# An MLP whose second product keeps partial sums in PSUM and fills four output blocks directly, and GpSimd without its gate at unit 1

## The reference

```python
def rmsnorm(x, g):
    y = xf * lax.rsqrt(jnp.mean(xf * xf, axis=-1, keepdims=True) + EPS)
    return (y * g.astype(jnp.float32)).astype(x.dtype)

def ffn(h, w1, w2):
    return jnp.square(jax.nn.relu(h @ w1)) @ w2

for layer in range(DEPTH):
    ...                                     # mixer, residual add
    hp = hp + ffn(rmsnorm(hp, norm_ffn[layer]), w_ffn1[layer], w_ffn2[layer])
    hs = hs + ffn(rmsnorm(hs, norm_ffn[layer]), w_ffn1[layer], w_ffn2[layer])
y_prompt = rmsnorm(hp, norm_final)
```

## Time and profile before

| | us |
|---|---|
| median of 3 runs | 2751.97 |
| runs, lowest to highest | 2749.49 to 2754.66 |
| profiled execution | 2746.19 |
| its span, first to last instruction | 2744.5 |
| TensorE busy | 2639.2 (96%) |
| VectorE busy | 1495.5 (54%) |
| GpSimd busy | 1447.0 (53%) |
| ScalarE busy | 946.2 (34%) |
| granted TensorE clock, mean | 0.990 |

### The profile page before, as it was taken

The page is one execution under the profiler, slowest core; times in us unless marked ns, Lnnn a source line. Parts: engine busy times, 40 slices in busy tenths (PEclk is TensorE's granted clock), DMA queues, the critical chain, the costliest instruction groups (busy, mean ns, idle before and its releaser), DMA issues. The chain is left out here.

```text
span 2744.5 us, 54327 instructions
## 1 busy us (share of the span) xinstructions
PE 2639.2 (96%) x22779; PEld 2521.7 (92%) x22779; DVE 1495.5 (54%) x1849; ACT 946.2 (34%) x1644; POOL 1447.0 (53%) x912
## 2 busy tenths in 40 slices
PE   8999989999999999999999998899999999999988
PEld 8999978986777799999999998899998999999988
DVE  5112186775554317455576769327336554676677
ACT  4100044656666324333333332211134333334332
POOL 6332201100001456777688888443548777688884
PEclk9999999999999999999999999999999999999999
DMA  6111243320204623344554431311223435554331
GB/s 194 47 48 63 93 145 109 95 77 2 94 2 140 234 74 139 116 163 153 184 213 146 155 117 31 131 47 47 94 108 108 148 113 166 201 216 152 126 109 63
DMA packets 197276, 319.98 MB, mean 117 GB/s; under 512 B 10813, under 2 KB 125250, under 8 KB 193898
## 3 DMA queue, kind: packets, MB, share of 16 engines
q1 hardware_dynamic: 186586, 293.37, 32.1%
q0 software_dynamic: 4032, 14.68, 1.5%
q10 hardware_dynamic: 6416, 8.45, 0.9%
HBM read 228.99 MB, written 91.67 MB: 117 GB/s over the span
## 5 line engine op out<-in xcount | busy, mean ns | idle before, releaser
L932 PE MATMUL psum<-part_hi,whl 128*128 128x258 f32 x3136 | 515.2, 286 | 23.8 <-DVE xlo_plain L1204 14.7
L932 PEld LDWEIGHTS psum<-part_hi,whl 128*128 128x128 f32 x3136 | 438.5, 191 | 27.5 <-DVE xlo_plain L1204 15.4
L478 PE MATMUL psum<-xhi,whl 128*128 128x344 f32 x1776 | 329.2, 320 | 1.1 <-ACT vCs L1367 0.6
L908 PE MATMUL psum<-shi,whl 128*128 128x258 f32 x1920 | 324.4, 283 | 2.2 <-DVE xlo_plain L1167 2.2
L932 PE MATMUL psum<-part_lo,whl 128*128 128x258 f32 x1568 | 317.0, 284 | 0.0
L449 POOL TENSOR_TENSOR whl<-wraw,zeroc 128x1024 fp32r<-128x1024 f32 x62 | 121.3, 1957 | 354.3 <-PE psum L478 169.0
L478 PEld LDWEIGHTS psum<-xhi,whl 128*128 128x128 f32 x1776 | 288.3, 188 | 1.7 <-issue 1.7
L908 PEld LDWEIGHTS psum<-shi,whl 128*128 128x128 f32 x1920 | 271.6, 190 | 2.6 <-POOL whl L353 2.6
L908 PE MATMUL psum<-xhi,whl 128*128 128x258 f32 x1440 | 250.5, 286 | 10.0 <-ACT xlo_plain L1047 10.0
L932 PEld LDWEIGHTS psum<-part_lo,whl 128*128 128x128 f32 x1568 | 244.8, 191 | 0.0
L353 POOL TENSOR_TENSOR whl<-raw_even,whl 128x512 fp32r<-128x512 f32 x112 | 175.5, 1581 | 86.3 <-ACT whl L974 62.2
(11 more groups left out here) (519 smaller groups left out, 5509.9 us busy)
## 6 DMA issues: line engine op xcount, KB each, us to landing
part_raw<-b_spill SPq DMA_DIRECT2D x98, 516.0 KB
b_spill<-rows_H SPq DMA_DIRECT2D x78, 516.0 KB, 3.9
rows<-in_cache_cmp_kv SPq DMA_DIRECT2D x128, 128.0 KB, 2.6
raw_even<-in_w_ffn SPq DMA_DIRECT2D x16, 1024.0 KB, 6.5
out_even<-in_w_ffn SPq DMA_DIRECT2D x16, 1024.0 KB, 6.2
out_odd<-in_w_ffn SPq DMA_DIRECT2D x16, 1024.0 KB, 7.7
raw_odd<-in_w_ffn SPq DMA_DIRECT2D x14, 1024.0 KB, 7.2
wraw<-in_w_in_ab SPq DMA_DIRECT2D x26, 512.0 KB, 3.6
```

What stands on the lines that cost most here:

```text
L478: last = pe.matmul(psum[:, 3 * bset + c, 0:TC], w, rhs[ah][:, k0 + k, c * TC:(c + 1) * TC], start=(k == 0 and n == 0), stop=(k == kn - 1 a ...
L908: last = pe.matmul(psum[:, 2 * pair + h, 0:QT], fast_weights(first, u, i, wh)[:, k, :], fast_operand(i, ah)[:, k, h * QT:(h + 1) * QT], st ...
L932: last = pe.matmul(psum[:, 2 * p + h, 0:QT], out_weights(first, n, wh)[:, k, p % 2, :], (part_hi, part_lo)[ah][x][:, k, h * QT:(h + 1) * Q ...
```

## The change

- `ORDER` becomes 0, 4, 6, 1, 2, 3, 5 and `PARTS` follows it. Block products 0, 4, 6, 1 are added up in PSUM, and so are 3 and 5: only products at places 0, 4 and 5 of a chunk start a new sum. VectorE writes each state after a product into one of four output blocks (`BLOCK`), as a copy for the first four of chunk 0 and as an addition otherwise.
- The joins on VectorE and GpSimd are gone, also GpSimd's wait for them ahead of the plain weights. Layer 1's last row is scaled from its output block.
- GpSimd's second sum goes to a scratch tile (`second_sum`), free once unit 15's product 0 is done, and the order of its parts is new.
- A plain tile is finished in PSUM: sum, factor and residual, the last into `hT`. `f_res` is gone; TensorE waits for `f_h`.
- In the first product GpSimd's order of a unit is low0, low1, low2, s1, low3, s3, s2, low4, s4, low5, low6, without the gate at unit 1. ScalarE's `high(1, 2)` stands right behind `high(1, 1)`.
- In unit 15 VectorE splits operand part 1 ahead of the last square.

```diff
@@ pool_fast
-                if u == 1:
-                    pool.wait_ge(sD, dve_at(layer, "s4_3"))
                 low(0, a11)
                 low(1, a22)
+                low(2, a12)
                 total("low1", a22, a21, a22, ALU.add)
+                low(3, a22)
                 total("s1", a21, a11, a21, ALU.subtract)
                 total("s3", a11, a22, a11, ALU.subtract)
-                low(2, a12)
-                total("low2", a12, a12, a11, ALU.subtract)
-                pool.wait_ge(v_pool, pool_at(layer, f"{u}.s4"))
-                low(3, a22)
                 low(4, a11)
+                total("s2", a12, a12, a11, ALU.subtract)
                 low(5, a12)
                 low(6, a21)
@@ pool_out
-                low(c, 1, 0)
-                low(c, 1, 1)
                 low(c, 0, 0)
                 low(c, 0, 1)
                 for g in range(2):
                     a11, a12, a21, a22 = blocks_[g]
-                    total(c, g, "low1", a22, a21, a22, ALU.add)
-                    total(c, g, "s1", a21, a11, a21, ALU.subtract)
-                    pool.wait_ge(v_pool, pool_at(layer, f"c{c}.low0_{g}"))
-                    total(c, g, "s3", a11, a22, a11, ALU.subtract)
+                    total(c, g, "low0", a11, a11, a21, ALU.subtract)
+                    if c == 0:
+                        pool.wait_ge(v_done, product_done(layer, 15, 0))
+                    total(c, g, "s3", second_sum(g), a22, a11, ALU.subtract)
                     low(c, 4, g)
...
-            pool.wait_ge(sD, dve_at(layer, "m6_4_3"))
-            pool.tensor_tensor(total_of(4), total_of(4), total_of(0), ALU.add).then_inc(v_pool, 1)
-            plain_low(0)
...
+            for q in range(8):
                 plain_low(q)
@@ orders
-        ORDER = (1, 0, 4, 6, 3, 2, 5)
-        PARTS = ("T4", "B11", "T2", "T3", "T1", "B21", "B22")
+        ORDER = (0, 4, 6, 1, 2, 3, 5)
+        PARTS = ("B11", "T2", "T3", "T4", "B21", "T1", "B22")
@@ places
+        BLOCK = {0: (0, 0), 4: (0, 1), 6: (1, 1), 1: (1, 0), 2: (0, 0), 3: (1, 1), 5: (0, 1)}
+        BEFORE = {2: 0, 5: 4, 3: 6}
+        AFTER = {0: 2, 4: 5, 6: 3, 1: 1}
@@ pe_ffn
-                                                     start=(k == 0 and m == 0), stop=(k == 1 and m == 2))
+                                                     start=(k == 0 and m == 0 and o in (0, 4, 5)),
+                                                     stop=(k == 1 and m == 2), skip_group_check=True)
...
-                    pe.wait_ge(f_res, F0 + 8 * layer + q - 1)
+                    pe.wait_ge(f_h, F0 + 8 * layer + q - 1)
@@ act_ffn
             high(1, 0)
             high(1, 1)
+            high(1, 2)
             sums_high(S_T1, "s1_3")
...
-            high(1, 2)
             first_relu(0)
@@ dve_ffn, the products
-                    if c == 0:
+                    if c == 0 and i not in BEFORE:
                         event(dve.tensor_copy(quarters(out_total(i, p)), two_banks(p)))
                     else:
-                        dve.wait_ge(sD, dve_at(layer, f"m{c - 1}_{i}_{p}"))
...
+                        if i in BEFORE:
+                            dve.wait_ge(sD, dve_at(layer, f"m{c}_{BEFORE[i]}_{p}"))
+                        else:
+                            dve.wait_ge(sD, dve_at(layer, f"m{c - 1}_{AFTER[i]}_{p}"))
...
-                if j == 44:
-                    dve.wait_ge(sD, dve_at(layer, "m6_0_3"))
-                    event(dve.tensor_tensor(total_of(2), total_of(2), total_of(0), ALU.add))
...
@@ dve_ffn, the tiles
-                dve.tensor_tensor(thirds(row), thirds(row), pset(n % 2), ALU.add).then_inc(f_res, 1)
-                dve.wait_ge(f_res, F0 + 8 * layer + n + 1)
-                s, v = link("dve", dve.tensor_tensor(row, row, fwide[:, :], ALU.mult))
+                dve.wait_ge(sD, dve_at(layer, f"m6_{(5, 3)[n % 2]}_{p}"))
+                s, v = link("dve", dve.tensor_tensor(pset(n % 2), pset(n % 2), thirds(out_row(n)), ALU.add))
+                dve.wait_ge(s, v)
+                s, v = link("dve", dve.tensor_tensor(pset(n % 2), pset(n % 2), thirds(fwide[:, :]), ALU.mult))
                 dve.wait_ge(s, v)
                 dve.wait_ge(s_reload[p], 32 if layer == 0 else 64)
-                dve.tensor_tensor(hT[:, n, :], hT[:, n, :], row, ALU.add).then_inc(f_h, 1)
+                dve.tensor_tensor(thirds(hT[:, n, :]), thirds(hT[:, n, :]), pset(n % 2), ALU.add).then_inc(f_h, 1)
@@ n_products_by_k
-                        pe.wait_ge(f_res, 7 + t // 3 + F0)
+                        pe.wait_ge(f_h, 7 + t // 3 + F0)
```

More of the change, by code:

```diff
@@ L391, in pool_out @@
             for c in range(7):
-                blocks_ = [[out_block(first, c, i, g) for i in (0, 2, 6, 1)] for g in range(2)]
-                low(c, 1, 0)
-                low(c, 1, 1)
+                blocks_ = [[out_block(first, c, i, g) for i in (0, 2, 3, 1)] for g in range(2)]
                 low(c, 0, 0)
@@ L729, in dve_mlp @@
                 order += ["g0"] if u == 15 else []
[L730 to L731 removed]
+                order += [f"c12_{u}", f"square0_{u}", f"u3_{u}", f"c21_{u}", f"c22_{u}"]
+                order += ["g1"] if u == 15 else []
+                order += [f"square1_{u}"]
+                order += [f"{x}_{u // 2}" for x in ("T1", "T2", "T4", "T3")] if u % 2 and u < 15 else []
             for j in range(49):
@@ L737, in dve_mlp @@
                 order += {47: ["g49", "g50"], 48: ["g52"]}.get(j, [f"g{j + 2}"])
-                order += {86 // 2 + 1: ["e11"], 86 // 2 + 2: ["e12a"], 86 // 2 + 3: ["e12b"]}.get(j, [])
             return order
-        POOL_UNIT = ("low0", "low1", "s1", "s3", "s2", "low2", "s4", "low3", "low4", "low5", "low6")
-        POOL_OUT = ("low1_0", "low1_1", "low0_0", "low0_1", "s1_0", "s3_0", "s2_0", "low4_0", "s1_1", "s3_1", "s2_1",
-                    "low4_1", "low6_0", "low6_1", "low3_0", "low3_1", "low2_0", "s4_0", "low2_1", "s4_1", "low5_0", "low5_1")
+        POOL_UNIT = ("low0", "low1", "low2", "s1", "low3", "s3", "s2", "low4", "s4", "low5", "low6")
+        POOL_OUT = ("low0_0", "low0_1", "s3_0", "s2_0", "low4_0", "s3_1", "s2_1", "low4_1", "low6_0", "low6_1",
+                    "low1_0", "low1_1", "s1_0", "s1_1", "low2_0", "s4_0", "low2_1", "s4_1", "low3_0", "low3_1", "low5_0", "low5_1")
         def pool_mlp():
@@ L747, in pool_mlp @@
             order += [f"c{c}.{x}" for c in range(7) for x in POOL_OUT]
-            order += ["V", "plain0", "U3", "plain1", "plain2", "plain3", "C21_0", "C22_0", "plain4", "plain5"]
-            order += [f"{x}_{p}" for p in range(1, 4) for x in ("C21", "C22")]
-            return order + ["plain6", "plain7", "scaled", "with_residual"]
+            return order + [f"plain{q}" for q in range(8)] + ["scaled", "with_residual"]
         def act_at(layer, name):
```

97 lines of the change are left out of this document (28 added, 69 removed).

## The result

The changed kernel takes 2758.15 us (median of 12 runs, 2752.56 to 2760.21), the kernel before, on the same chip, 2749.05 (12 runs, 2744.35 to 2754.66). The ratio is 1.0035 with a 95% interval of 1.0027 to 1.0043: 9 us slower, where 9 us faster was forecast. The profiled execution has a span of 2757.3 us (before 2744.5) and a granted clock of 0.985 (before 0.990).

The account below looks back on a forecast made before the run. TensorE's stalls and the clock behind them were taken to bound the kernel. Gains of 35.4 us less losses of 24.6 and 2 made it 8.8 us faster: 2743 us against a median of 2751.97, range 2726 to 2762.

Parts of the forecast that it names:

- What bounds the kernel: Whole kernel: TensorE is busy 96% of the span; only about 100 us of it, not matmuls, can be won.
- Second product: Joins between the last accumulations go: stalls of 10.3 us in layer 0, 8.6 in layer 1, about 2 of clock each.
- End of layer 0: Plain tiles finished in PSUM: waits inside tiles go and those behind the last shrink, 10.2 us gained with the clock.
- the clock: End of layer 0: with a wait of only 2.7 us behind the last tile, 3.2 us of half-speed loss counted as saved.
- Rival 4: Plain tiles of layer 0: PSUM operands as slow as contended SBUF ones, 4.3 us lost per tile, 2776 us; chance 0.03.
- rival 3: Second product: another late thing uses the joins' cover, half of 18.9 us stay, 2752 us; chance 0.14.
- Unit 1: First product: ScalarE's early third split delays unit 1's start and third product; loss 12.3 us a layer, 24.6 in two.
- Rival 2: Unit 1: ScalarE's wait costs nothing, the 24.6 us fall away, 2718 us; chance 0.06.
- Units 2 to 15: First product: GpSimd's new chain across units is slightly late, 0.15 us at every second of 28 changes; 2 us lost.
- rival 1: Unit changes: the chain is late everywhere, measurably slower from 0.6 us per change, 2763 us at 0.8; chance 0.13.

Follow-up runs that it names:

- b4_both_back_gate: Changed kernel with the whole first product as before (ScalarE's split, GpSimd's order and gate), second product as changed: 2710.2 us, ratio 0.9857.
- b3_both_back: Changed kernel with GpSimd's order and ScalarE's third split of the first product as before, still without GpSimd's gate: 2715.4 us, ratio 0.9881.
- c3_hidden_sums_zero: Changed kernel with VectorE's four sums of hidden rows behind every second unit replaced by zeros, new GpSimd order kept: ratio 0.9946.
- d4_first_product_alone: Kernel before with only the three first-product edits (no gate, GpSimd's new order, early third split): 46.1 us slower, ratio 1.0174.
- d3_before_no_joins: Kernel before without its thirteen joining instructions (three VectorE, ten GpSimd) in each layer, output incomplete: ratio 0.9902.

## Why the prediction was wrong

**What bounds the kernel.** Right: all gains and losses are stalls of TensorE and the clock behind them.

**Second product.** Right in place and nearly in size: 14.3 us in each layer against 12.2 and 11.7. No new wait came in the last six products. The stalls at the start became 1.1 us shorter, which is the size that was set, but by luck. GpSimd's was to fall from 1.3 to 0.2 us and fell from 1.26 to 0.97; VectorE's was to stay and fell from 2.09 to 1.26.

**End of layer 0.** Right: three PSUM instructions of 1.24, 1.24 and 1.23 us where 1.25 was taken, tiles without stalls, and 2.80 us behind the last where 2.7 was worked out. One term failed: the clock. I counted its 3.2 us as saved since the wait would be under 4.7 us; it fell to 0.50 behind the 2.80 in the profile of after all the same, and in seven of the nine experiments that have this stall. Where it didn't the tail takes 67.4 us, where it did once about 68.9 for the same work and the same stall, so this costs 1.5 us. In after and in `b4_both_back_gate` the tail takes 70.5: a second half-speed stretch of 3.4 us stands 13.6 us behind the first, with no stall ahead of it, and what brought it stays open. The tiles made up for most of this: they became 5.0 us shorter (50.5 to 45.5), where 3.9 was forecast. Rival 4 is out, and rival 3 too: nothing took the joins' cover.

**Unit 1.** Right, and the reason for the largest part of the loss: idle 8.38 us against 9.0 ahead of the first product, then 6.98 and 6.16 in the two layers against about 6, the third product 12.0 us late against 12.3. GpSimd's five instructions in the chain took 10.3 us, as summed. The forecast put it all on ScalarE's wait in its headline and yet counted GpSimd's order in its sum; the runs make the order the larger part (6.9 and 7.2 us, the split 3.9 and 5.0). Rival 2 is out. One sentence was wrong without harm here: that nobody waits for what GpSimd starts sooner without its gate. `b3_both_back` shows 2.66 us of it, which ScalarE's longer wait covers in the changed kernel.

**Units 2 to 15.** This step failed, and with it the sign. It set 2 us for both layers together, 1 for each. Measured are 11.9 and 11.4 us:
- from unit 3 on 7.2 us in each layer, all from the six stalls of 0.96 at full clock, where the forecast had 0.15 at each of 14 changes in both layers. Each costs 1.2 us, more than its idle time: the matmul behind it doesn't overlap with the one ahead (0.16 us otherwise), and two of them take 0.48 us instead of 0.40;
- unit 2 with 4.7 and 4.2 us, which no step had: its stall is 3.73 instead of 1.22 and 1.00 us, 2.5 and 2.7 more, and the rest is the half-speed stretch behind it.

The prices in the chain's arithmetic came out nearly right: 13.2 us alone, 15.2 contended, against 14.6 of time. Counted from the start of the product behind the one that frees the third place, the chain ended 13.8 us later without the contention (`c3_hidden_sums_zero`), 15.4 with it, and TensorE wanted it at 14.5. The seven GpSimd instructions took 11.5 us in the contended chain, where seven at 1.59 make 11.1. This is the mean of a mixture, 2.2 and 2.3 us for two of them and 1.3 to 1.8 for the rest. What failed is the step from there to the 0.15: the contended case, 0.6 too long by the forecast's own sum, was written down to 0.15 with the sentence "VectorE's work on SBUF fills little of this time". That holds for the weights of even units and is false for those of odd ones: beside them five VectorE instructions on SBUF run, 11 us in a row (the square and the four sums), and each change to an odd unit from 5 on pays the full 1.2 us. In the kernel before GpSimd makes its three sums together, ahead of the third low part, and the same VectorE instructions bring no stall at these places.

So rival 1 was the right mechanism. It came at every second unit, with 0.5 us of time a change on average, below the 0.6 that it had been given as its point of decision, and unit 2 brought the rest.

In sum: second products and tail gained 39.3 us where the forecast had 35.4, and the first products lost 47.6 where it had 26.6, of which unit 1 has 24.3 against 24.6 and units 2 to 15 have 23.3 against 2.

## What to carry to other kernels

Where GpSimd and a second engine hand work back and forth, put everything that doesn't wait for the other engine ahead of what does. A chain across units is to be costed separately for each kind of unit that VectorE's work makes, with the contended price wherever that work stands beside it; a mean over both kinds hid a loss that every second unit pays in full. In a change of two halves, take the half that gains: here the second product alone gave 39 us, and two moves of instructions that stood ahead of awaited ones gave some 12 more.

## What the runs showed of the hardware

- VectorE and GpSimd stretch each other when VectorE reads two operands in SBUF: a GpSimd low part of 128x512 from 1.30 to 2.26 us, VectorE's sum of 128x1032 from 1.23 to 2.2, its multiplication from 1.23 to 3.35. Beside VectorE's reciprocal of 6.59 us, with one SBUF operand, GpSimd's instructions took 1.26 to 1.28 us, and beside its memsets 1.29. With one SBUF operand and the other in PSUM VectorE stayed at 1.24 us, though GpSimd ran an addition of the norm beside the two instructions at 1711.05 and 1712.33 shown above:

```profile
1711.38 2.41 POOL L569 TENSOR_TENSOR acc<-acc,sqb 128x1032 f32<-128x1032 f32 x1 [3.26 <-ACT sqb L561]
```

  The Trainium skill (GPSIMD Engine Reference, Specifications) says that the two share interfaces to SBUF and collide where VectorE has two SBUF inputs; the rows of both kinds agree (2.26 and 3.35 us with two, 1.24 with one).
- Writing a 128x1032 result to PSUM costs VectorE no more than writing it to SBUF (1.24 and 1.22 us).
- The length of a stall alone doesn't tell whether the clock falls behind it. The same stall of 2.80 us was followed by a fall in eight profiles and by none in two. At unit 2 stalls of 1.57 us and less were followed by none, those of 3.2 to 3.7 us always by one. The stall of 2.08 to 2.13 us at the start of the second product was followed by one in three of seven cases (both layers of `d4_first_product_alone`, layer 0 of `c3_hidden_sums_zero`; not in the kernel before nor in `d3_before_no_joins`). So the clock's price at a stall of 2.8 us is 0 or 1.5 us, and what decides it stays open.
